# A two-block transformer kernel on one core: the first mixer starts from the rows, and its unused inputs load later

## The reference

```python
h = h + gla_mixer(rms_norm(h, attn_norm[0]), gla_w_in, gla_w_gate_up, gla_b_gate, gla_head_norm, gla_w_out)

def gla_mixer(h, w_in, w_gate_up, b_gate, g_head, w_out):
    q, k, v, g_lr, r = split(h @ w_in)              # 512, 512, 1024, 16, 1024 columns
    log_a = log_sigmoid(g_lr @ w_gate_up + b_gate) / 16
    b = cumsum of log_a inside each chunk of 64 tokens
    q_dec, k_inv, k_end = q * exp(b) / sqrt(128), k * exp(-b), k * exp(b_end - b)
    o = attention inside a chunk + state carried over chunks, from q_dec, k_inv, k_end, v
    o = rms_norm(o, g_head) * silu(r)
    return o @ w_out
```

## Time and profile before

| | us |
|---|---|
| median of three runs | 2925.28 |
| the profiled execution, its own time | 2923.5 |
| its span, first to last instruction | 2921.7 |
| TensorE busy (matmul) | 2722.8 (93%) |
| VectorE busy | 575.8 (20%) |
| ScalarE busy | 356.4 (12%) |
| GpSimd busy | 85.7 (3%) |
| mean granted TensorE clock | 0.979 |

### The profile page before, as it was taken

One profiled execution on the slowest core, in us unless ns is written; L12 is line 12 of the kernel. 1 busy time (PEld: TensorE's weight loads), 2 busy tenths in 40 slices (PEclk: granted clock), 3 DMA queues, 4 the chain that ended last, 5 costly groups with the idle time before them and its releaser, 6 DMA issues. The chain is left out here.

```text
span 2921.7 us, 70140 instructions
## 1 busy us (share of the span) xinstructions
PE 2722.8 (93%) x31522; PEld 1995.3 (68%) x31522; DVE 575.8 (20%) x1423; ACT 356.4 (12%) x896; POOL 85.7 (3%) x130
## 2 busy tenths in 40 slices
PE   6889999988899999999998898989999999898999
PEld 3758856658899899999896446865444444555883
DVE  0120001112000000001002224742222201232331
ACT  1010001001000000000002121221111100131110
POOL 0000000000000000000000002200000000000000
PEclk9999999989999999999998999999999999999999
DMA  8663435629999999999991110002222222302432
GB/s 348 258 248 146 156 130 204 257 87 342 364 405 417 392 407 420 411 402 419 400 418 76 43 72 30 3 2 72 79 80 72 72 87 79 119 18 83 148 144 86
DMA packets 80391, 583.94 MB, mean 200 GB/s; under 512 B 8912, under 2 KB 8912, under 8 KB 10064
## 3 DMA queue, kind: packets, MB, share of 16 engines
q1 hardware_dynamic: 79920, 580.15, 50.7%
q10 hardware_dynamic: 288, 1.05, 0.1%
HBM read 580.11 MB, written 1.05 MB: 199 GB/s over the span
## 5 line engine op out<-in xcount | busy, mean ns | idle before, releaser
L1471 PE MATMUL ps<-arena,ring 128*64 128x80 f32 x14336 | 509.5, 234 | 39.1 <-issue 36.1
L1471 PEld LDWEIGHTS ps<-arena,ring 128*64 128x64 f32 x14336 | 503.3, 138 | 44.6 <-issue 42.9
L2830 PE MATMUL ps<-hT,ring 128*128 128x256 f32 (+2 forms) x1472 | 455.3, 472 | 5.6 <-ACT hT L472 3.4
L2830 PEld LDWEIGHTS ps<-hT,ring 128*128 128x128 f32 x1472 | 274.5, 190 | 185.2 <-issue 166.3
L359 PE MATMUL ps<-ring,arena 128*128 128x512 f32 x896 | 390.7, 597 | 4.9 <-DVE arena L2735 3.8
L359 PEld LDWEIGHTS ps<-ring,arena 128*128 128x128 f32 x896 | 171.0, 192 | 218.4 <-issue 212.2
L1480 PE MATMUL ps<-arena,ring 128*64 128x80 f32 x7168 | 255.8, 234 | 19.4 <-issue 19.3
L1480 PEld LDWEIGHTS ps<-arena,ring 128*64 128x64 f32 x7168 | 251.9, 138 | 22.2 <-issue 21.9
L981 PE MATMUL ps<-hT,ring 128*128 128x256 f32 (+1 forms) x736 | 152.7, 370 | 2.6 <-ACT hT L470 2.6
L1621 DVE TENSOR_TENSOR arena<-arena,ps 128x80 f32<-128x80 f32 x224 | 53.2, 237 | 486.9 <-ACT arena L1600 486.8
L981 PEld LDWEIGHTS ps<-hT,ring 128*128 128x128 f32 x736 | 134.8, 190 | 20.3 <-issue 3.0
(11 more groups left out here) (469 smaller groups left out, 2153.5 us busy)
## 6 DMA issues: line engine op xcount, KB each, us to landing
ring<-in_stream SPq DMA_DIRECT2D x547, 1024.0 KB, 7.8
par<-in_params SPq DMA_DIRECT2D x1, 3397.0 KB, 29.3
h<-in_x ACTq DMA_DIRECT2D x2, 512.0 KB, 7.8
cx<-in_ctx SPq DMA_DIRECT2D x2, 512.0 KB, 30.4
out<-h SPq DMA_DIRECT2D x4, 256.0 KB, 2.0
par<-in_params SPq DMA_DIRECT2D x1, 941.0 KB, 5.9
```

The source lines that it names most:

```text
L1471: last = nc.tensor.matmul(ps[m:m + 64, up_bank[j], half * P:half * P + CAP], w[:, k, half * P + m:half * P + m + 64], hTe[:, k, :], start= ...
L2830: last = nc.tensor.matmul(ps[:, 2 * BANKS_CONV[f % RING] + half, tok], w[:, k, half * P:half * P + P], hT[:, k, tok], start=(k == 0), stop ...
```

## The change

The rows x are loaded first, on SyncE's queue, each token tile with a semaphore of its own. The identity and the gain (136 columns, `now`) come on ScalarE's queue, the other early parameters behind x. The norm is written for one token tile at a time (`first_norm`), with four banks in place of three; it waits for its own inputs only. The ada turn that stood ahead of it is gone from there. A value tile is now one step, and the first of them waits for each token tile separately. One ada turn stands in the gate group, in its ninth round, and the other seven in the group of q, k and r. The tail of `params` and the context are sent behind weight tile 41 (`load_turns(sp, 1, 6)`) in place of behind tile 6.

```diff
-            first = where["first"]
-            sp.dma_start(par[:, 0:first], params[:, 0:first]).then_inc(params_in, 16)
+            now, first = where["now"], where["first"]
+            for t in range(TT):
+                sp.dma_start(h[:, t, :], out["x"][t * P:t * P + P, :]).then_inc(x_in[t], 16)
+            sp.dma_start(par[:, now:first], params[:, now:first]).then_inc(params_in, 16)
             for t in range(RING):
                 sp.dma_start(ring[:, t, :], stream[t]).then_inc(landed[t], 16)
+        def load_rest(sp):
+            first = where["first"]
             sp.dma_start(par[:, first:width], params[:, first:width]).then_inc(rest_in, 16)
             for t in range(TT):
                 sp.dma_start(cx[:, t, :], out["ctx"][t * P:t * P + P, :]).then_inc(rest_in, 16)
...
+        def first_norm(gain, scratch, at=0):
+            known = []
+            def total(t):
+                @block.vector
+                def _(dve):
+                    dve.wait_ge(act_done.sem, act_done.n)
+                    dve_done.by(nc.vector.tensor_scalar(small[:, at + 2 + t:at + 3 + t], small[:, at + t:at + t + 1], 1.0 / D,
+                                                        EPS, ALU.mult, ALU.add))
+                @block.gpsimd
+                def _(pool):
+                    pool.wait_ge(dve_done.sem, dve_done.n)
+                    pool.wait_ge(pool_done.sem, pool_done.n)
+                    inverse_root(pool, small[:, at + 4 + t:at + 5 + t], small[:, at + 2 + t:at + 3 + t])
...
+            def square(t):
                 @block.scalar
                 def _(act):
-                    after_all(act)
-                    link(act, act_done, nc.scalar.activation(scratch[:, t, :], x[:, t, :], ACT.Square,
+                    act.wait_ge(x_in[t], 16)
+                    link(act, act_done, nc.scalar.activation(scratch[:, t, :], h[:, t, :], ACT.Square,
                                                              accum_out=small[:, at + t:at + t + 1]))
...
+            def turned(t):
                 @block.vector
                 def _(dve):
+                    if t == 0:
+                        dve.wait_ge(ident_in, 16)
                     dve.wait_ge(pool_done.sem, pool_done.n)
-                    o, i_ = (scratch[:, t, :], x[:, t, :]) if keep else (scratch[:, t, 0:P], ident)
-                    link(dve, dve_done, nc.vector.tensor_scalar(o, i_, small[:, at + 4 + t:at + 5 + t], None,
-                                                                ALU.mult))
+                    link(dve, dve_done, nc.vector.tensor_scalar(scratch[:, t, 0:P], ident, small[:, at + 4 + t:at + 5 + t],
+                                                                None, ALU.mult))
                 for q in range(2):
-                    b = bank0 + (2 * t + q) % 3
                     @block.tensor
                     def _(pe):
-                        claim(pe, b)
+                        if q == 0:
+                            pe.wait_ge(x_in[t], 16)
                         pe.wait_ge(dve_done.sem, dve_done.n)
                         for j in range(4):
                             cols = slice((4 * q + j) * P, (4 * q + j + 1) * P)
-                            o = ps[:, b, j * P:j * P + P]
-                            if keep:
-                                last = nc.tensor.transpose(o, scratch[:, t, cols], ident)
-                            else:
-                                last = nc.tensor.matmul(o, x[:, t, cols], scratch[:, t, 0:P], start=True, stop=True)
+                            last = nc.tensor.matmul(ps[:, 2 * t + q, j * P:j * P + P], h[:, t, cols], scratch[:, t, 0:P],
+                                                    start=True, stop=True)
                         pe_done.by(last)
+                return pe_done.n
...
+            def columns(t, mark):
+                ready = []
                 for q in range(2):
-                    b = bank0 + (2 * t + q) % 3
+                    b = 2 * t + q
                     @(block.vector, block.scalar)[q]
                     def _(eng):
...
+                        if q == 1 and t == 0:
+                            eng.wait_ge(ident_in, 16)
+                        eng.wait_ge(pe_done.sem, mark - 1 + q)
+                        for j in range(4):
+                            k = 4 * q + j
+                            o, i_, g = hT[:, k, t * P:t * P + P], ps[:, b, j * P:j * P + P], gain[:, k:k + 1]
+                            if q == 0:
+                                ins = nc.vector.tensor_scalar(o, i_, g, None, ALU.mult)
+                            else:
+                                ins = nc.scalar.activation(o, i_, ACT.Copy, scale=g)
                         done = (dve_done, act_done)[q]
                         freed[b] = [(done, done.by(ins))]
-                yield
+                        ready.append((done, done.n))
+                return ready
+            square(0)
+            total(0)
+            square(1)
+            first = turned(0)
+            total(1)
+            known.append(columns(0, first))
+            second = turned(1)
+            known.append(columns(1, second))
+            return known
...
-            for t in range(TT):
-                act.dma_start(h[:, t, :], out["x"][t * P:t * P + P, :]).then_inc(x_in, 16)
+            now = where["now"]
+            act.dma_start(par[:, 0:now], params[:, 0:now]).then_inc(ident_in, 16)
...
-        for eng in (block.tensor, block.scalar, block.vector, block.gpsimd):
-            @eng
-            def _(e):
-                e.wait_ge(params_in, 16)
-                e.wait_ge(x_in, 16 * TT)
...
+        def at_rounds(lane, rounds):
+            for n in range(max(rounds) + 1):
+                if n in rounds:
+                    next(lane)
+                yield
...
-        def gate_steps():
+        def gate_steps(ready):
...
-        def value_steps():
-            @block.tensor
-            def _(pe):
-                after_all(pe)
+        def value_steps(ready):
             for n in range(2):
-                token_rows([4, 5], hT, 0, KT, kind="gla_v")
-                for t in range(TT):
-                    copy_bank(4 + t, v[:, t, n * 512:n * 512 + 512])
-                yield
-                yield
+                for half in range(2):
+                    @block.tensor
+                    def _(pe):
+                        if half == 0:
+                            claim(pe, 4, 5)
+                        w = weights(pe, "gla_v").rearrange("p (k n) -> p k n", k=4)
+                        for t in range(TT):
+                            if n == half == 0:
+                                wait_marks(pe, ready[t])
+                            for k in range(4 * half, 4 * half + 4):
+                                last = nc.tensor.matmul(ps[:, 4 + t, :], hT[:, k, t * P:t * P + P], w[:, k - 4 * half, :],
+                                                        start=(k == 0), stop=(k == KT - 1))
+                        tile_used.by(last)
+                    if half == 1:
+                        for t in range(TT):
+                            copy_bank(4 + t, v[:, t, n * 512:n * 512 + 512])
+                    for _ in range((1, 2, 3, 0)[2 * n + half]):
+                        yield
...
         ada_turns = ada_lane()
-        side_by_side([norm_T_steps(h, [(hT, c("attn0"), None)], 0, xs), some(ada_turns, 1, 2)])
-        side_by_side([gate_steps(), value_steps(), some(ada_turns, 1, 2)])
+        ready = first_norm(c("attn0"), xs)
+        silu_of_cond()
+        for eng in (block.tensor, block.scalar, block.vector, block.gpsimd):
+            @eng
+            def _(e):
+                e.wait_ge(params_in, 16)
+        side_by_side([value_steps(ready), gate_steps(ready), at_rounds(ada_turns, (8,))])
         side_by_side([gla_steps(), some(ada_turns, 48 // LANES, 2)])
...
-            load_turns(sp, 1, moe_turn)
+            load_turns(sp, 1, 6)
+            load_rest(sp)
+            load_turns(sp, 6, moe_turn)
...
-    early = ["ident", "ones", "cond", "attn0", "ada_b", "w_glr", "gate_up", "gate_b", "gla_sum", "gla_mask", "gla_head"]
+    early = ["ident", "attn0", "ones", "cond", "ada_b", "w_glr", "gate_up", "gate_b", "gla_sum", "gla_mask", "gla_head"]
     out = {name: out[name] for name in early} | out
-    where, at = {"first": sum(out[name].shape[1] for name in early)}, 0
+    where, at = {"first": sum(out[name].shape[1] for name in early), "now": sum(out[name].shape[1] for name in early[:2])}, 0
```

More of the change, by code:

```diff
@@ L88, in build @@
         landed = [sem(f"landed{i}") for i in range(RING)]
+        ident_in = sem("ident_in")
         params_in = sem("params_in")
         rest_in = sem("rest_in")
-        x_in = sem("x_in")
+        x_in = [sem(f"x_in{t}") for t in range(TT)]
         stored = sem("stored")
@@ L223, in inverse_root @@
             link(pool, pool_done, nc.gpsimd.tensor_tensor(out_, in_, half_pow[:, 0:in_.shape[1]], ALU.pow))
```

(24 more changed lines are left out.)

31 lines of the change are left out of this document (10 added, 21 removed).

## The result

| | before | changed | ratio, 95% interval |
|---|---|---|---|
| first comparison, medians | 2925.15 | 2903.20 | 0.9923, 0.9906 to 0.9940 |
| second | 2922.71 | 2903.56 | 0.9942, 0.9927 to 0.9957 |
| third | 2924.12 | 2906.95 | 0.9934, 0.9916 to 0.9952 |
| profiled executions | 2923.5, 2920.2, 2921.05 | 2905.77, 2900.25, 2909.03 | |

The change is faster, by 0.6 to 0.8%: 22.0 us by the medians of the first comparison, 19.2 and 17.2 in two later ones with the same programs. Forecast were 14.1. Single runs spread more than the first three showed: the kernel before ran in 2914.7 to 2932.5, the changed one in 2900.2 to 2912.2. One more execution of the changed kernel, in the third comparison, took 11054.8 and is left out of its row.

A forecast was written before the change was run, and what follows sets the result against it. TensorE, busy 93% of the span, was taken as the bound, with four gaps in the first 191 us. First q tile 27.0 earlier, less 12.9 at the mixer's end, gives 14.1: 2925.3 - 14.1 = 2911, range 2903 to 2918.

The forecast's parts named there:

- First value tile at 13.3 to 15.0, taken 13.8: Start of the mixer: first turning of rows at 7.3 on a cold TensorE, then the first value tile at 13.8.
- Cost 12.9: End of the mixer: loss from the last ada turn standing behind the first output turning, 7.6 of waiting plus 5.3.
- The gate gap: Ahead of the gate products: a new TensorE wait of 2.0, since VectorE copies the banks before the low-rank result.
- The 8.6 of the third value tile: Behind the gate products: the third value tile takes 8.6, as the clock falls again; ends at 46.9.
- the possible 1: In the q, k, r products: the second ada turn waits for its fourth weight tile, nothing, or 1 if slow.
- from there on all rows shifted by one number: From the output projection, near 177, to the end: every later row comes earlier by the same amount.
- (a): End of the mixer: late transfers hide, only the ada turn is paid; gain 22, 2903; chance 0.14, shared with everything well.
- (b): Gate products: the clock does not fall, 3.3 more gain, 2907.5; within the forecast's spread, no chance of its own.
- (c): End of the mixer: wait for tile 43 and output weights about 20, gain 2, 2923; chance 0.05 together with (e).
- (d): Split value tiles: TensorE never reaches full clock among them, 3.4 slower, 2929; chance 0.03.
- (e): Before slice 10: a stage waits for weights and the earlier start is given back; chance 0.05 together with (c).
- two readings for the clock at the projection: Output projection: it starts cold after transposes, sum 14.1, or the ada turn is near enough to keep it fast, 16.2.

## Why the prediction was right and wrong

The direction was right, and in the mixer the mechanism came out step by step: the new gaps, the place of the last ada turn, its wait for tile 43. The size was too small: 14.1 against 22.0 in the first comparison. Two things did it.

The smaller one is the sum for the mixer, 14.1 against 16.5 in the first profile (15.1 over three). "First value tile at 13.3 to 15.0, taken 13.8": it was 12.73, below its lower bound, since both row tiles were turned in 5.5 and not in 6.0 or more. The gate gap was 1.75, not 2.0, and the first q tile took 7.15, so 28.3 were gained at its end where I had 27.0. "Cost 12.9" was 11.3 (6.75 of wait and 5.02, with 5.0 from there to the projection in place of 5.5), and 0.4 of the possible 1 went to the second ada turn. Nearly each miss was on the kind side. The 8.6 of the third value tile was the other way, and from the earlier trace rows it should have been 6.9 and 2.05, so 9.0; it took 9.1 up to the sums.

The larger one is the step behind the mixer: "from there on all rows shifted by one number", with the 1.8 between one profiled execution and the median of three runs as all that lies between executions, and a range made only of terms of the mixer. The prediction named its own sign of being wrong, a shift at the output projection that is not that at the end. Against the first profile of before, the three profiles of the changed kernel were 16.5, 13.3 and 14.6 ahead at the projection, and 17.7, 23.3 and 14.5 at the end. The three runs of before lay within 2.5 us by luck. 106 runs of the kernel before lie within 17.8 (standard deviation 3.7), and the profiles show where: an untouched stretch of weight streaming takes 871.0 to 880.5, and falls of the clock behind it add or take 3 to 5. The first comparison was at the kind end of this, the third (17.2) closer to the sum measured in the mixer. The sum was right within 1 to 2.5 at the projection; behind it 1.5 more were gained on average by the profiles, and 2.4 beyond these by all runs together, whose place is open. The range of 2903 to 2918 for a median of four runs was too narrow by this spread, and its edge was where the first median fell.

Of the rivals, (a) fell: the late transfers do not hide, and undoing them gave 7.4. I had (a) at 22, and 22.0 is what was measured first, for another reason: the number agreed by chance, and a time alone would have confirmed (a). (b) fell in every profile of the changed kernel (the clock did fall), and came true in one of the two programs with two ada turns in the gate group, not in the other; what decides between them is open. (c), (d) and (e) did not come. Of the two readings for the clock at the projection neither was whole: it fell again for 3.4 us at 174.4 although the ada turn had ended at 169.8, and the gain was 0.6. By the Trainium skill, "TensorE: Matmul & The Clock Gate", section "Part 4: PE-mode transpose", transposes do not count as busy for the clock in the way of other products. The trace agrees in that the twelve transposes between did not keep it up, but it doesn't show this by itself: TensorE was also idle for 2.6 of these 4.6 us.

What each part gave, from experiments that undo it: rows first 8.7 at the first q tile, the value tiles between the gate's products 8.4, and the late transfers minus 7 at the end. The moved ada turn alone gives 4.8 in the kernel before. These are 21.9 of the 26.5 at the first q tile. Putting a second turn back ahead of the q tile cost 0 to 0.9 (59.46 and 60.46). The norm by token tile was not tried by itself, and such parts need not add up, so the other 4.6 are open.

## What to carry to other kernels

A transfer that nobody needs yet belongs into a stretch in which the ring is full, not behind the last tile that looks harmless. Here the queue moved 92 GB/s from 28 to 51 us and was the bound at 158. An item moved in a round-robin order arrives elsewhere too: taking one ada turn from the start pushed the last one over the edge of the wait that had hidden it, and putting one back brought the projection 4.8 forward (164.04 against 168.83). Before a range is given, ask for more runs than three, or look for a long stretch in which the memory queues are busy all the time, and add its spread.

## What the runs showed of the hardware

The same 7168 and 14336 products at the weight stream's full rate took 871.0 to 880.5 us in fourteen profiles. The products of 16 and of 1 rows went with a fall of the clock in or behind them in thirteen of the fourteen profiles, with a gap ahead of them or without (granted clock 0.75 from 31.9 to 37.0 in the changed kernel). 68 KB in 544-byte rows ahead of the rows of x on one queue went with a landing 2.3 us later. 4.5 MB issued between tiles 41 and 42 put 13.5 us between their landings (148.7 and 162.2). Of the start, 7.26 us are left until TensorE can turn the first row tile.
